# First expert block of a gathered mixture-of-experts stage: its own row and index buffers, two gathers issued together, and the second block's row transposes placed ahead of the first up products

## What is computed

```python
def _moe(h, router_g, router_e, w1, w3, w2):
    # every token is routed to TOP_K = 2 of 32 experts, each with a gate
    ...
    order = jnp.argsort(e_flat)                 # the tokens sorted by expert
    ...                                         # padded to whole blocks of one expert each
    def block(args):
        tok, e = args
        xb = h[tok]                             # gather the block's rows
        return (jax.nn.silu(xb @ w1[e]) * (xb @ w3[e])) @ w2[e]
    out = lax.map(block, ...)
    y = zeros.at[slot_tok].add(out * slot_w)    # scatter-add, times the gate
```

## Time and profile before

| | |
|---|---|
| median of 3 runs | 1651.77 us (1650.79 to 1654.41) |
| the profiled execution's own time | 1653.96 us |
| its span, first to last instruction | 1652.1 us |
| mean granted clock of TensorE | 0.949 of full |
| TensorE busy | 1492.8 us, 90% of the span |
| DMA, mean over the span | 199 GB/s |

### The profile page before, as it was taken

How to read it: one execution, slowest core, us unless ns; L and a number is a source line. 1 busy time by engine, 2 the same in 40 slices (tenths; PEclk the granted TensorE clock), 3 DMA queues, 4 the chain that set the end, 5 groups by cost and what they waited for, 6 DMA issues and landing times. The chain is left out here.

```text
span 1652.1 us, 34622 instructions
## 1 busy us (share of the span) xinstructions
PE 1492.8 (90%) x14240; PEld 979.9 (59%) x14240; DVE 538.9 (33%) x1269; ACT 435.4 (26%) x1227; POOL 290.3 (18%) x250
## 2 busy tenths in 40 slices
PE   8999999989998999999998767999999999999850
PEld 4666666657666777777776433666666655555520
DVE  2444544423234544455443260111111111111106
ACT  2211111121114344444342100223222222222214
POOL 0000000012124343244332000111111111111105
PEclk9999999989998999999999878999999999999975
DMA  7333233252416122221111197999999999999925
GB/s 259 82 93 74 63 79 81 55 161 66 125 57 232 33 77 103 103 84 70 68 69 39 64 412 254 366 380 378 383 376 383 372 383 377 376 379 386 323 71 216
DMA packets 119251, 328.42 MB, mean 199 GB/s; under 512 B 42712, under 2 KB 72328, under 8 KB 92552
## 3 DMA queue, kind: packets, MB, share of 16 engines
q1 hardware_dynamic: 110296, 300.59, 49.2%
q0 software_dynamic: 7728, 22.29, 5.8%
q10 hardware_dynamic: 1152, 4.52, 0.7%
HBM read 284.08 MB, written 48.14 MB: 201 GB/s over the span
## 5 line engine op out<-in xcount | busy, mean ns | idle before, releaser
L2172 PE MATMUL bank<-sb_arena 128*32 128x256 f32 x6336 | 360.3, 388 | 17.1 <-DMA sb_arena<-w 16.1
L397 PE MATMUL bank<-sb_arena 128*128 128x368 f32 x1056 | 330.6, 476 | 6.7 <-DMA sb_arena<-xT 6.7
L2172 PEld LDWEIGHTS bank<-sb_arena 128*32 128x32 f32 x6336 | 205.7, 112 | 160.7 <-DMA sb_arena<-w 18.2
L397 PEld LDWEIGHTS bank<-sb_arena 128*128 128x128 f32 x1056 | 201.7, 191 | 133.5 <-DMA sb_arena<-w_conv 6.6
L2195 PE MATMUL bank<-sb_arena 128*32 128x256 f32 x3168 | 179.2, 382 | 10.5 <-DMA sb_arena<-w 10.5
L2195 PEld LDWEIGHTS bank<-sb_arena 128*32 128x32 f32 x3168 | 103.1, 111 | 81.0 <-issue 14.3
L984 PE MATMUL bank<-sb_arena 128*128 128x512 f32 (+1 forms) x288 | 131.2, 595 | 6.3 <-DVE sb_rlog L1595 5.0
L2138 POOL DMA_INDIRECT d_acc<-sb_arena,sb_oidx x32 | 46.2, 1443 | 479.2 <-ACT sb_arena L2256 479.2
L2306 DVE SCALAR_TENSOR_TENSOR sb_arena<-sb_arena,bank 128x128 f32<-128x128 f32 x99 | 28.5, 288 | 304.4 <-ACT sb_arena L2242 304.4
L2242 ACT ACTIVATE sb_arena<-bank 128x128 f32<-128x128 f32 x99 | 27.4, 277 | 361.1 <-PE bank L2172 361.1
L781 PE MATMUL bank<-sb_arena 128*128 128x384 f32 (+1 forms) x288 | 96.5, 488 | 7.7 <-PEq L150 7.7
(11 more groups left out here) (345 smaller groups left out, 1749.8 us busy)
## 6 DMA issues: line engine op xcount, KB each, us to landing
sb_arena<-w SPq DMA_DIRECT2D x198, 1024.0 KB, 30.5
sb_arena<-w_conv SPq DMA_DIRECT2D x28, 512.0 KB, 4.6
sb_arena<-d_conv SPq DMA_DIRECT2D x7, 1792.0 KB, 7.3
d_conv<-sb_arena SPq DMA_DIRECT2D x22, 512.0 KB, 3.3
sb_arena<-d_gam SPq DMA_DIRECT2D x8, 768.0 KB, 4.1
d_x<-sb_arena SPq DMA_DIRECT2D x9, 512.0 KB, 2.6
sb_arena<-xT ACTq DMA_DIRECT2D x8, 552.0 KB, 9.5
sb_arena<-w_out SPq DMA_DIRECT2D x8, 512.0 KB, 7.4
```

What stands on the lines that cost most here:

```text
L397: last = e.matmul(bank[3 * r + s][:, 0:TN], wring[n % NV][:, k, :], xT[:, k, TN * s:TN * s + TN], start=(k == 0), stop=(k == KT - 1))
L2172: mm = e.matmul(bank[r][j * CG:(j + 1) * CG, 0:2 * P], xgT[:, k, g * CG:(g + 1) * CG], w13[s][quarter_of(j, r)][:, k, :], start=(k == 0), ...
```

## The change

The first block gets a row buffer `xg_first` and an index buffer `idx_first` of its own, with two semaphores (`e_if`, `e_xf`). VectorE fills `idx_first` first of all, zeroes both row buffers, and takes the second block's index into `idx` at once. GpSimd issues both gathers one behind the other, ahead of the plain DMA. TensorE transposes the second block's rows before up(0), not after it. `e_idx` starts at 1, and every count of `e_x` is one gather less.

```diff
-START.update({"e_eo": 3})
+START.update({"e_eo": 3, "e_idx": 1})
...
         xg = A(P, D)
+        xg_first = A(P, D)
...
         idx = sb("idx", [BLK, 1], I32)
+        idx_first = sb("idx_first", [BLK, 1], I32)
...
                 e.wait_ge(S["e_clr"], 1)
-                gather(1)
+                e.wait_ge(S["e_if"], 1)
+                e.indirect_dma_start(xg_first[0:BLK], None, a["d_x1"], bass.IndirectOffsetOnAxis(ap=idx_first[:, 0:1], axis=0),
+                                     bounds_check=TO - 1, oob_is_err=False).then_inc(S["e_xf"], 16)
+                gather(2)
                 e.dma_start(a["d_acc"][TO:TO + BLK, :], eo[0:BLK]).then_inc(S["e_st"], 16)
-                gather(2)
                 gather(3)
...
                 def x_transpose(n, first=False):
-                    e.wait_ge(S["e_x"], 16 * n + 16)
-                    if not first:
+                    if first:
+                        e.wait_ge(S["e_xf"], 16)
+                    else:
+                        e.wait_ge(S["e_x"], 16 * n)
                         e.wait_ge(S["e_xT"], n)
+                    src = xg_first if first else xg
                     for k in range(KT):
-                        mm = e.transpose(..., xg[0:BLK, k * P:(k + 1) * P], ident[0:BLK, 0:BLK])
+                        mm = e.transpose(..., src[0:BLK, k * P:(k + 1) * P], ident[0:BLK, 0:BLK])
...
                 x_transpose(0, first=True)
                 e.wait_ge(S["e_xT"], 1)
+                x_transpose(1)
                 up(0, 0, 1)
-                x_transpose(1)
...
-                e.wait_ge(S["e_x"], 16 * last + 48)
+                e.wait_ge(S["e_x"], 16 * last + 32)
...
                 def take(n, first=False):
                     at = place(n)
                     if not first:
-                        e.wait_ge(S["e_x"], 16 * n)
+                        e.wait_ge(S["e_x"], 16 * n - 16)
                         e.wait_ge(S["e_xT_ps"], n)
...
+                at = place(0)
+                e.tensor_scalar(idx_first[:], slot[0:BLK, bass.ds(at, 1)], 1.0, None, ALU.mult).then_inc(S["e_if"], 1)
+                e.memset(xg_first, 0.0)
                 e.memset(xg, 0.0).then_inc(S["e_clr"], 1)
-                take(0, first=True)
+                take(1, first=True)
                 e.memset(eo, 0.0).then_inc(S["e_go"], 1)
-                take(1)
                 gate(0, first=True)
                 take(2)
```

More of the change, by code:

```diff
@@ L2073, in program @@
         idx = sb("idx", [BLK, 1], I32)
+        idx_first = sb("idx_first", [BLK, 1], I32)
         oidx = sb("oidx", [BLK, 1], I32)
         oidx_last = sb("oidx_last", [BLK, 1], I32)
-        sem("e_idx", "e_x", "e_xT_ps", "e_xT", "e_up", "e_th", "e_s", "e_hm", "e_hT_ps", "e_hT", "e_out", "e_ev", "e_eo", "e_og", "e_st", "e_go", "e_clr")
+        sem("e_idx", "e_x", "e_xf", "e_if", "e_xT_ps", "e_xT", "e_up", "e_th", "e_s", "e_hm", "e_hT_ps", "e_hT", "e_out", "e_ev", "e_eo", "e_og", "e_st", "e_go", "e_clr")
         def group_of(j, r):
@@ L2157, in x_transpose @@
                 def x_transpose(n, first=False):
-                    e.wait_ge(S["e_x"], 16 * n + 16)
-                    if not first:
+                    if first:
+                        e.wait_ge(S["e_xf"], 16)
+                    else:
+                        e.wait_ge(S["e_x"], 16 * n)
                         e.wait_ge(S["e_xT"], n)
+                    src = xg_first if first else xg
                     for k in range(KT):
-                        mm = e.transpose(bank[3 + k // 4][:, (k % 4) * BLK:(k % 4 + 1) * BLK], xg[0:BLK, k * P:(k + 1) * P], ident[0:BLK, 0:BLK])
+                        mm = e.transpose(bank[3 + k // 4][:, (k % 4) * BLK:(k % 4 + 1) * BLK], src[0:BLK, k * P:(k + 1) * P], ident[0:BLK, 0:BLK])
                     mm.then_inc(S["e_xT_ps"], 1)
```

## The result

The changed kernel takes 1656.07 us (median of 20 runs, 1651.39 to 1660.02), the kernel before 1653.36 us in the same measurement (20 runs, 1647.73 to 1656.53). The ratio is 1.0021, 95% interval 1.0012 to 1.0029: 3.5 us more, between 2.0 and 4.8 (the two medians alone differ by 2.7). The sum had said 1.7 us, and the likeliest case "no change that can be told". It is slower, by an amount that lies at the very edge of what a measurement tells. Three executions of the kernels of this document took 2131 to 5891 us and count in no ratio; the profiled one of e4_warm was among them.

A forecast was written before the change was run, and what follows sets the result against it. TensorE was taken to set the pace up to 1340 us, the weights' transfers after. Head +0.4 and second gather with transposes +2.4, less 1.3 from the clock, plus 0.2 for the median's clock gave +1.7 us: 1653.5 us, range 1650.0 to 1656.5.

The forecast's parts named there:

- The sum: Whole kernel: head, second gather and transposes, clock return and clock of the median add to +1.7 us; bounds +0.3 to +3.2.
- the likeliest case: Whole kernel: the measured time stays within about 0.2%, 3.3 us, of no change; chance 0.72.
- the bound, the place and the sign: Expert stage: TensorE, then weights' transfers set the pace; delay ahead of up(1) reaches the end one to one; slower, +1.7 us.
- the removal of x_transpose(1) from behind up(0): TensorE behind up(0): costed at nothing, though it took 0.88 us, as TensorE is idle for 7.62 us in any case.
- The case that the shift does not reach the end: Stream of weights: slack behind its hole takes the delay up, time stays 1651.8 us; chance 0.12.
- The fast case: Second gather lands with the first or within the copy, clock stays up or rises at once; -3.5 us, 1648.3; chance 0.08.
- what the clock gives back: TensorE in up(0): the clock rises earlier, so up(0) loses 1.5 us in place of 2.76; 1.3 us returned.
- VectorE's head: VectorE ahead of the first gather: filling and copying the first block's index delays its release by +0.4 us, bounds 0 to 0.7.
- Second gather: GpSimd's queue: lands at 997.9, 2.8 us behind the first; with its transposes ahead of up(0) at half clock, +2.4 us.
- Third gather: Ahead of x_transpose(2): 6.8 us to landing, issued 2.5 us behind up(0)'s end as before; the 7.62 us wait stays.
- slower beyond measure: Rival at up(0) and up(1): second gather lands later than about 999.3, clock falls again; +4.3 us, 1656.1; chance 0.2.
- the port: VectorE's memset of `eo` beside GpSimd's first gather: no cost by the rule; if locked out, at most 0.5 us, 1654.0; chance 0.05.

The follow-up runs named there:

- e4_warm: Changed kernel with 11 idle products in place of 8 ahead of x_transpose(0) and 2 more behind it; 1655.24 us, ratio 1.0024 to the kernel before.
- e3_between: Changed kernel with the plain DMA of 384 KB put between the two gathers on GpSimd; 1659.24 us, ratio 1.0047 to the kernel before.
- e5_warm_look: The kernel of e4_warm run once more for its trace only; no ratio of its own, x_transpose(2) at +38.43 us from the first idle product.
- e7_two: Changed kernel with own buffers for the second block too, three gathers at once, x_transpose(1) behind up(0), one memset ahead; 1645.01 us, ratio 0.9949 to before.
- e6_defer: Changed kernel with the last 4 MB of the third expert's weights issued only when the second gather has landed; 1650.74 us, ratio 0.9989 to before.
- e10_before_defer: Kernel before with only the last 4 MB of the third expert's weights issued late, behind the first gather's landing; 1651.62 us, ratio 0.9985.
- e1_back: Changed kernel with x_transpose(1) put behind up(0) again, own buffers and two gathers together kept; ratio 1.0008 to the kernel before.
- e2_take: Changed kernel with take(2) moved ahead of gate(0) on VectorE; 1647.48 us, ratio 0.9971 to the kernel before.

## Why the prediction was right or wrong

**Right: the bound, the place and the sign.** The chain behind the first hole in the stream of weights passes the shift on to the end, or most of it; the table bears it out for the gains in times and traces, for the losses in the times alone. take(2) stayed behind gate(0), the third gather's wait stayed (7.13 us), and the removal of x_transpose(1) from behind up(0) was worth nothing (h_transpose(0) starts 1.2 us behind the end of up(0) in both, waiting for VectorE). The case that the shift does not reach the end is out by the interval, which starts at 2.0 us, though the two profiled executions by themselves look like it. The fast case is out too: the second gather landed 3.7 us behind the first, not with it.

**Wrong: the size, and with it the likeliest case.** The step that failed is the term of the second gather, taken from the row of a plain DMA; what the clock gives back came out too large beside it. The sum gave +1.5 us in the profiled execution where the trace shows +3.2, and the case that time stays within 0.2% was given most of the chance, though its upper bound of +3.2 was all but that limit. Term by term:

- *VectorE's head.* Forecast +0.4; the first gather was issued 0.65 us later (+3.91 against +3.26). The register load was bare, as I took it (3.06 us of issue ahead of VectorE's first instruction, 2.52 before). Besides, the copy took 0.15 us in place of 0.1, and 0.16 us of issue stood ahead of each of the two memsets.
- *Second gather.* Forecast at the issue of the first + 1.18, and 2.8 us behind its landing, from the plain DMA's 10.2 us. It was issued 1.48 us behind (0.30 of issue between two gathers) and took 11.0 us. Together with the head x_transpose(1) began at +16.51 in place of +15.04. This is the largest miss, 1.5 us, of which 0.25 is the head, 0.2 the first gather (8.8 us in place of 8.6) and 0.9 the distance of the second behind it, 3.7 us in place of 2.8. A plain DMA was the wrong stand-in: in e3_between one lands 2.9 us behind the first gather again. The 11.6 us of a gather beside the full stream were the nearer row, which the prediction kept for the bound only.
- *What the clock gives back.* Forecast 1.3 us in up(0); the trace shows 0.5 (12.84 against 13.33). And e4_warm, by the trace of e5_warm_look, shows how little such a return is worth here: with the clock kept full 2.6 us came back at the end of up(0), but 1.2 at x_transpose(2) and 0.55 behind up(1).
- *Third gather.* Forecast 6.8 us, measured 6.3: 0.5 the other way.

The errors, 1.5 and 0.8 less 0.5, make up the 1.7 between +1.5 and +3.2, to 0.1. The head, the second gather and the clock all erred to the same side. The rival "slower beyond measure" named the landing later than 999.3 (+16.4) as the point from which it decides, and the second gather landed at +16.4. Its other half did not come: up(1) took 11.50 us, as before. That its 1656.1 us is the measured time is chance, since it was counted from a median of 1651.77 us and the kernel before took 1653.36 in this measurement. So is it that the high bound of the sum, +3.2, is the shift in the trace: its terms were others.

**The ring order and the port.** Of the rule of the Trainium skill (DMA: Bandwidth & Descriptors, Queues, rings and completion order) that a DMA engine consumes a queue's descriptors in ring order (the section says it of the queues of SP and ScalarE, and not of GpSimd's), e3_between and e7_two show for GpSimd's queue what the trace of before could only suggest: one transfer more ahead of a gather delays it by 2.6 us, 0.6 of it in its issue, and two more behind it by 0.2 to 0.5 us. The rule of the Trainium skill on VectorE's port (SBUF — State Buffer, Who interferes with whom), by which the memset of `eo` adds nothing, agrees with the traces. In the changed kernel the memset lies beside the first gather's issue for its first 0.15 us only. In e7_two memsets run beside nearly all of both issues (989.24 to 990.15 beside the first, at 988.93, and 990.36 to 991.27 beside the second, at 990.41), which take 1.18 and 0.97 us, where such issues without one took 1.18 and 0.96.

## What to carry to other kernels

An early fetch only helps if the instruction that asks for the next one moves with it: look for the first wait behind the edit, and for what releases its transfer, before costing anything else. Here a gather's time to landing was a price of what ran beside it (4 us alone, 9 to 11 beside the stream). In a kernel like this one, put the latency-bound transfer first and let the bulk wait those few microseconds. And never let the first block's products stand behind the second block's data; give it a buffer of its own, or make sure that the data is there.

## What the runs showed that was not expected

- A gather of 96 rows of 4 KB lands 4.1 us after issue when no weights move, and a second one issued 1.5 us later in 5.1 us (e6_defer, with the last 4 MB held back); beside the stream they take 8.8 and 11.0. In e7_two the fourth transfer in the queue landed 15.7 us after its issue.
- Holding back 4 MB of a stream that seems to bound the whole stage gained 2.5 to 7 us in four pairs of kernels: the stream stands still anyway while it waits for up(0) (5 GB/s for 6 us in the changed kernel). Its price was a later third gather where one was waited for (9.1 and 8.6 us to landing in e6_defer and e10_before_defer, in place of 6.3 and 6.8).
- The time to landing of the third gather, the one that is waited for, spreads from 6.3 us (changed kernel) over 6.9 (e1_back) and 7.7 (e5_warm_look) though the weights are asked for at the same distances ahead of it in all three. Issued while the stream stands still, in e2_take, it lands in 4.1 us.
